# Encoder trunk: decay products one pair later, the second norm's gain and offset inside the output projection, and the first weight unit split in halves

## The reference, cut to what matters

```
proj = x @ W_in                      # q/k/v, z, beta, decay, window q/k/v, gates
branch A: centred conv (5 taps) + SiLU on q/k/v, L2-normed q/k,
          gated delta rule forward and backward, per-head gated norm
          beta = sigmoid(b);  g = -exp(a_log) * softplus(a + dt_bias), cumulated per chunk
branch B: windowed attention with rotary q/k and a sink
merged = sigmoid(gate_A) * (A @ W_A) + sigmoid(gate_B) * (B @ W_B)
x = LayerNorm(alpha * x + merged @ W_out)       # first norm, gain and offset ln1
x = LayerNorm(alpha * x + SwiGLU(x))            # second norm, gain and offset ln2
```

## Time and profile before

| | |
|---|---|
| runs | 2651.22, 2661.05, 2661.07 us |
| profiled execution | 2658.32 us, its span 2656.5 us, mean granted TensorE clock 0.974 |
| PE busy | 2421.4 us (91%), 14128 matmuls |
| DVE / ACT / POOL busy | 1272.7 / 762.7 / 1061.5 us |
| DMA | 169.72 MB, mean 64 GB/s |

### The profile page before, as it was taken

One profiled execution on the slowest core, in us unless ns is written; L12 is line 12 of the kernel. 1 busy time (PEld: TensorE's weight loads), 2 busy tenths in 40 slices (PEclk: granted clock), 3 DMA queues, 4 the chain that ended last, 5 costly groups with the idle time before them and its releaser, 6 DMA issues. The chain is left out here.

```text
span 2656.5 us, 35272 instructions
## 1 busy us (share of the span) xinstructions
PE 2421.4 (91%) x14128; PEld 1987.6 (75%) x14128; DVE 1272.7 (48%) x2262; ACT 762.7 (29%) x2050; POOL 1061.5 (40%) x612
## 2 busy tenths in 40 slices
PE   7988999987999989999989889999969999899997
PEld 5876777776887868888767677777758878788886
DVE  3667778756433251110257778787564432511102
ACT  2544444422332021110035344444223320211100
POOL 3541111142115646666635411111521156466665
PEclk8999999998999999999989899999989999899999
DMA  3220000021002323333212100000210032233332
GB/s 120 88 64 25 25 25 25 25 72 40 25 25 95 99 68 96 95 99 116 89 56 80 56 25 25 25 25 25 80 32 25 32 99 93 72 97 102 102 105 87
DMA packets 47249, 169.72 MB, mean 64 GB/s; under 512 B 5872, under 2 KB 6384, under 8 KB 46960
## 3 DMA queue, kind: packets, MB, share of 16 engines
q1 hardware_dynamic: 44496, 160.71, 19.3%
q10 hardware_dynamic: 2592, 6.76, 0.7%
HBM read 165.36 MB, written 2.10 MB: 63 GB/s over the span
## 5 line engine op out<-in xcount | busy, mean ns | idle before, releaser
L435 POOL TENSOR_SCALAR wh<-w_raw 128x1024 fp32r<-128x1024 f32 x300 | 325.5, 1085 | 1543.5 <-DMA w_raw<-stream 1543.5
L437 POOL TENSOR_TENSOR wl<-w_raw,wh 128x1024 fp32r<-128x1024 f32 x300 | 724.5, 2415 | 25.0
L462 PE MATMUL PS<-xh,wh 128*128 128x512 f32 x1472 | 610.6, 415 | 26.5 <-POOL wl L437 10.0
L464 PE MATMUL PS<-xl,wh 128*128 128x512 f32 x1472 | 583.0, 396 | 0.0
L463 PE MATMUL PS<-xh,wl 128*128 128x512 f32 x1472 | 581.5, 395 | 0.0
L462 PEld LDWEIGHTS PS<-xh,wh 128*128 128x128 f32 x1472 | 282.1, 192 | 79.3 <-POOL wl L437 14.6
L464 PEld LDWEIGHTS PS<-xl,wh 128*128 128x128 f32 x1472 | 280.9, 191 | 61.1
L463 PEld LDWEIGHTS PS<-xh,wl 128*128 128x128 f32 x1472 | 282.7, 192 | 48.5
L1420 DVE SCALAR_TENSOR_TENSOR conv_acc<-PS,cw,conv_acc 128x510 f32<-128x510 f32 x192 | 143.8, 749 | 122.4 <-ACT conv_acc L1019 117.1
L1787 DVE TENSOR_TENSOR hf<-sg,PS 128x512 f32<-128x512 f32 x44 | 30.2, 687 | 358.0 <-PE PS L464 358.0
L1684 DVE SCALAR_TENSOR_TENSOR x<-x,PS 128x1024 f32<-128x1024 f32 x12 | 14.6, 1219 | 292.3 <-PE PS L464 292.3
(11 more groups left out here) (258 smaller groups left out, 4391.8 us busy)
## 6 DMA issues: line engine op xcount, KB each, us to landing
w_raw<-stream SPq DMA_DIRECT2D x300, 512.0 KB, 3.5
ln_g<-ln_rows ACTq DMA_DIRECT2D x4, 512.0 KB, 4.3
ln_b<-ln_rows ACTq DMA_DIRECT2D x4, 512.0 KB, 5.4
out<-x SPq DMA_DIRECT2D x3, 512.0 KB, 2.6
cst<-consts ACTq DMA_DIRECT2D x1, 1216.0 KB, 13.0
x<-x_in SPq DMA_DIRECT2D x2, 512.0 KB, 5.5
x<-x_in ACTq DMA_DIRECT2D x2, 512.0 KB, 7.5
out<-x SPq DMA_DIRECT2D x2, 256.0 KB, 2.1
```

The costliest lines, as they stand in the source:

```text
L435: nc.gpsimd.tensor_scalar(wh[s][:], w_raw[s][:], 1.0, 1.0, ALU.mult, ALU.mult).then_inc(w_hi_done, 1)
L437: nc.gpsimd.tensor_tensor(wl[s][:], w_raw[s][:], wh[s][:].bitcast(F32), ALU.subtract).then_inc(split_done, 1)
L462: mm(o, ah, bh, start=first, stop=False)
L464: return mm(o, ah, bl, start=False, stop=last)
```

## The change

- SP loads `ba_raw` behind the third unit of a layer instead of ahead of the first, and POOL splits it there.
- POOL splits the very first unit in two halves; PE's `feature_pair` waits for each half, and for its second unit only at that unit's first step.
- The steps of the decays move: PE's turn from behind i = 1 to behind i = 2, PE's sums from behind i = 4 into i = 6 behind unit 0; DVE's inputs to i = 3, rates to 5, tables to 6, signs to 8; ACT's Exp to i = 4, Ln and Sigmoid to i = 5, exponents to i = 7.
- In `store_normed` ACT writes the first high part before it scales tile 2.
- The gain and offset of layer 0's second norm leave the pairs of layer 1 and run in one go behind layer 1's merge, before `norm(0)`. Their rows are loaded in front of layer 1's first norm; ACT waits for the eight operations and then loads the rows of that norm.

```diff
@@ SP
-                sp.dma_start(ba_raw[:], w_ba[l, :, :, :]).then_inc(ba_loaded, 16)
                 for u in range(l * UNITS, (l + 1) * UNITS):
                     s = u % SLOTS
+                    if u == l * UNITS + SLOTS:
+                        sp.dma_start(ba_raw[:], w_ba[l, :, :, :]).then_inc(ba_loaded, 16)
@@ POOL (the split of ba_raw becomes split_ba, otherwise as before)
+                    if u == l * UNITS + SLOTS:
+                        split_ba()
                     pool.wait_ge(loaded[s], u // SLOTS * 16 + 16)
                     settle(pool)
-                    nc.gpsimd.tensor_scalar(wh[s][:], w_raw[s][:], 1.0, 1.0, ALU.mult, ALU.mult).then_inc(w_hi_done, 1)
-                    pool.wait_ge(w_hi_done, u + 1)
-                    nc.gpsimd.tensor_tensor(wl[s][:], w_raw[s][:], wh[s][:].bitcast(F32),
-                                            ALU.subtract).then_inc(split_done, 1)
+                    parts = (slice(0, 512), slice(512, 1024)) if u == 0 else (slice(0, 1024),)
+                    for n, w in enumerate(parts):
+                        nc.gpsimd.tensor_scalar(wh[s][:, w], w_raw[s][:, w], 1.0, 1.0, ALU.mult,
+                                                ALU.mult).then_inc(w_hi_done, 1)
+                        pool.wait_ge(w_hi_done, u + n + 1 + (u > 0))
+                        nc.gpsimd.tensor_tensor(wl[s][:, w], w_raw[s][:, w], wh[s][:, w].bitcast(F32),
+                                                ALU.subtract).then_inc(split_done, 1)
@@ PE
-                pe.wait_ge(split_done, pair * 2 + s + 1)
+                pe.wait_ge(split_done, pair * 2 + s + 2)
@@ feature_pair, step(n, k)
+                    if first_pair == n == 0:
+                        pe.wait_ge(split_done, 1 if k < KT // 2 else 2)
+                    elif k == 0:
+                        unit_ready(first_pair, n)
@@ PE, pairs
                         qkv_turn(i - 1, s)
+                        if i == 6 and s == 0:
+                            decay_sums()
...
-                    if i == 1:
+                    if i == 2:
                         decay_inputs()
-                    if i == 4:
-                        decay_sums()
@@ ACT, store_normed
                 scaled(0)
+                high_part(0)
                 scaled(2)
-                high_part(0)
@@ ACT, pairs (decay_logs holds the Ln and the Sigmoid)
-                    if i == 3:
+                    if i == 4:
                         decay_curves()
-                    if i == 6:
+                    if i == 5:
+                        decay_logs()
+                    if i == 7:
                         decay_exponents()
@@ ACT, ahead of normed(0)
-                act.dma_start(ln_g[:], ln_rows[l, 0, :].partition_broadcast(P)).then_inc(ln_loaded, 16)
-                act.dma_start(ln_b[:], ln_rows[l, 1, :].partition_broadcast(P)).then_inc(ln_loaded, 16)
+                def norm_rows(l, n):
+                    act.dma_start(ln_g[:], ln_rows[l, n * 2, :].partition_broadcast(P)).then_inc(ln_loaded, 16)
+                    act.dma_start(ln_b[:], ln_rows[l, n * 2 + 1, :].partition_broadcast(P)).then_inc(ln_loaded, 16)
+                if l > 0:
+                    norm_rows(l - 1, 1)
+                    act.wait_ge(x_affine, (l * 2 - 1) * 8 + 8)
+                norm_rows(l, 0)
@@ ACT, ahead of normed(1): the loads of rows 2 and 3 become
+                if l == DEPTH - 1:
+                    norm_rows(l, 1)
@@ DVE, pairs
-                    if l > 0 and 3 <= i <= 6:
-                        output_gain(l - 1, 1, i - 3)
-                    if l > 0 and 7 <= i <= 10:
-                        output_offset(l - 1, 1, i - 7)
-                    if i == 2:
+                    if i == 3:
                         decay_inputs()
-                    if i == 3:
+                    if i == 5:
                         decay_rates()
-                    if i == 5:
+                    if i == 6:
                         decay_tables()
-                    if i == 6:
+                    if i == 8:
                         decay_signs()
-                    if i == 8:
                         key_norms()
@@ DVE, behind the merge
+                if l > 0:
+                    for c in range(CHUNKS):
+                        output_gain(l - 1, 1, c)
+                    for c in range(CHUNKS):
+                        output_offset(l - 1, 1, c)
                 norm(0)
```

More of the change, by code:

```diff
@@ L423, in _, with split_ba @@
             for l in range(0, DEPTH):
[L425 to L430, removed]
+                def split_ba():
+                    pool.wait_ge(ba_loaded, l * 16 + 16)
+                    settle(pool)
+                    flat = [t[:].rearrange("p k n -> p (k n)") for t in (ba_raw, bah, bal)]
+                    nc.gpsimd.tensor_scalar(flat[1], flat[0], 1.0, 1.0, ALU.mult, ALU.mult).then_inc(ba_split, 1)
+                    pool.wait_ge(ba_split, l * 2 + 1)
+                    nc.gpsimd.tensor_tensor(flat[2], flat[0], flat[1].bitcast(F32), ALU.subtract).then_inc(ba_split, 1)
                 for u in range(l * UNITS, (l + 1) * UNITS):
                     s = u % SLOTS
+                    if u == l * UNITS + SLOTS:
+                        split_ba()
                     pool.wait_ge(loaded[s], u // SLOTS * 16 + 16)
                     settle(pool)
-                    nc.gpsimd.tensor_scalar(wh[s][:], w_raw[s][:], 1.0, 1.0, ALU.mult, ALU.mult).then_inc(w_hi_done, 1)
-                    pool.wait_ge(w_hi_done, u + 1)
-                    nc.gpsimd.tensor_tensor(wl[s][:], w_raw[s][:], wh[s][:].bitcast(F32),
-                                            ALU.subtract).then_inc(split_done, 1)
+                    parts = (slice(0, 512), slice(512, 1024)) if u == 0 else (slice(0, 1024),)
[5 more added lines that the diff above has]
+                                                ALU.subtract).then_inc(split_done, 1)
             pool.wait_ge(ln_loaded, DEPTH * 64)
@@ L472, in feature_unit, with feature_pair @@
                 ins.then_inc(unit_done, 1)
-            def feature_pair(slots, lo_count):
+            def feature_pair(first_pair, lo_count):
+                slots = [slot_of(first_pair, n) for n in range(2)]
                 def step(n, k):
+                    if first_pair == n == 0:
+                        pe.wait_ge(split_done, 1 if k < KT // 2 else 2)
+                    elif k == 0:
+                        unit_ready(first_pair, n)
                     c = slice(k * P, (k + 1) * P)
@@ L565, in qkv_turn @@
                     ins.then_inc(tok_ready, 1)
-                feature_pair([unit_ready(l * PAIRS + AT_QKV, s) for s in range(2)], l * 16)
+                feature_pair(l * PAIRS + AT_QKV, l * 16)
                 pe.wait_ge(ready_bf, 7)
@@ L928, in _ @@
                         if i == j == 0:
-                            feature_pair([unit_ready(pair, s) for s in range(2)], l * 16 + 8)
+                            feature_pair(pair, l * 16 + 8)
                             continue
@@ L1000, in decay_curves, with decay_logs @@
                     A(sm[3][:], sm[2][:], ACT.Exp).then_inc(gate_act, 1)
+                def decay_logs():
                     act.wait_ge(gate_dve, l * 19 + 5)
@@ L1245, in _ @@
                           ACT.Copy).then_inc(ff_hi, 1)
-                act.dma_start(ln_g[:], ln_rows[l, 2, :].partition_broadcast(P)).then_inc(ln_loaded, 16)
-                act.dma_start(ln_b[:], ln_rows[l, 3, :].partition_broadcast(P)).then_inc(ln_loaded, 16)
+                if l == DEPTH - 1:
+                    norm_rows(l, 1)
                 normed(1)
```

## The result

The changed kernel took 2642.05 us as the median of 6 runs (2638.05 to 2647.63), the kernel before 2660.95 us beside it (6 runs, 2651.22 to 2665.48). The ratio is 0.9936, 95% interval 0.9920 to 0.9952: 17 us or 0.64% faster (18.9 us by the two medians). In two later jobs it gave 0.9919 (0.9902 to 0.9936) and 0.9928 (0.9903 to 0.9953). The forecast was 2644 us in a range of 2631 to 2655. So the sign, the time and the range held. One term of the sum, the burst, was wrong all the same, and losses that the sum did not have took its place.

What follows compares the result with a forecast made beforehand. PE, busy 91% of 2656.5 us, was taken as the bound, so only its gaps and the low clock behind them pay. 15.2 + 10.9 + 1.4 - 6.0 + 1.4 + 0.1 - 8.3 = 14.7 us below 2658.3 gave 2644, range 2631 to 2655.

Steps and rivals of the forecast that it cites:

- the burst: Layer 1's output projection: eight DVE products in one run hold POOL's subtraction off, PE stalls; 8.3 us lost.
- Decay turn: First stage, both layers: a pair later, PE's wait on `baT` and the low clock behind it vanish; 15.2 us saved.
- Gains out of the convs: Layer 1's convs: without gains and offsets its turns go as layer 0's; 10.9 us saved.
- Pair 4: Conv of pair 4, both layers: splitting ACT's three decay curves over two pairs ends its delay; 1.4 us saved.
- Decay sums: Pair 6, both layers: new 2.2 us wait before unit (6,1) plus 0.8 us for low clock; 6.0 us lost.
- Start: Kernel start: PE does six matmuls on the first half unit, then waits for unit 1; 1.4 us saved.
- Norm order: Three norms: first high part before the second scaling; earlier DVE subtraction waits longer for POOL; 0.1 us saved in all.
- rival (a): Output projection: POOL goes in between DVE's operations, so the 8.3 us loss goes; 2635 us, chance 0.30.
- the norm's run: Same eight operations behind the FFN's norm: POOL's operation took 2.54 us, starting at the run's end; evidence for the 8.3 us.
- the product row: Layer 1's convs: POOL's subtraction between two TMP products took only 2.68 us, so it went in between; evidence for (a).

Runs made afterwards that it cites:

- experiment 2: Changed kernel with the decay steps of PE, ACT and DVE back in their old places: 2648.56 us, 0.9958 of the kernel before.
- experiment 1: Changed kernel with the second norm's gains and offsets back in layer 1's convs, with their row loads: 2647.64 us, 0.9956 of the kernel before.
- experiment 4: Changed kernel with each layer's first norm's gains and offsets applied twice, sixteen DVE operations in one run: 2655.99 us, one execution.
- experiment 5: Changed kernel with DVE's run of eight in the output projection started only after POOL split the third weight unit: 2646.83 us, 0.9956 of the kernel before.
- job 2: Changed kernel run again unchanged, beside other versions on one chip: 2637.73 us median of 6 runs; profiled span 2631.2 us.
- job 3: Changed kernel run again unchanged, beside other versions on one chip: 2641.92 us median of 6 runs.
- Experiment 7: Changed kernel with DVE's last low part of the gated output moved behind the window copies: 2637.34 us, 0.9912 of the kernel before.

## Why the prediction was right, and where it was not

**Decay turn (15.2).** Right, in idle time and low clock: 7.6 and 7.8 us by the n-th matmul, 7.2 and 7.0 the other way round in experiment 2. It went whole, since nothing was late in its place.

**Gains out of the convs (10.9).** Right in mechanism and size: 5.6 + 5.8 = 11.4 in the first pair of traces, which holds pair 4 of layer 1 as well; 11.1 the other way round in experiment 1. Comparing layer 1 with layer 0 at the same place was what gave the number.

**Pair 4 (1.4).** 0.4 in layer 0, PE's wait of 0.43 us on the conv, for 0.7; within the sum above in layer 1.

**Decay sums (-6.0).** The wait was there in both layers, 1.88 and 1.82 us for 2.2. Low clock behind it did not come in this execution (1.00); in the two others of this kernel one short stretch followed in layer 0, none in layer 1. So 3.7 to 5 us for 6.0.

**Start (1.4).** PE began when foretold and waited until 17.93; 0.8 us was left, because the clock behind the new gap was 0.54. Over the three profiled executions of the changed kernel it was 0.8 to 2.2 us, over all twelve with this start 0.4 to 2.2.

**Norm order (0.1).** About nothing, as foretold. The first low part comes earlier and waits longer for POOL (2.55 for 1.99 us). PE's first unit behind the norms comes 0.5 us sooner in all than in before, from the last matmul ahead of each norm; 0.3 of this is layer 1's, where before lost time to low clock. Against the old order in the changed kernel it comes 0.2 us later in all. Both lie inside the bounds.

**The burst (-8.3).** This step failed. "POOL's subtraction waits from 2222.2 to 2231.2" and "PE stalls 5.9 us" did not come; DVE's eight operations took 19 us, POOL's operations 1 us more each, and PE lost 0.7 us at the last pair. It was rival (a)'s outcome. I had carried the behaviour of the earlier trace rows to another place because the operations were the same. They were, and experiment 4 shows that the behaviour in that place is real, with 11.58 us. But in the projection POOL gets its turn at each boundary, also when it comes in mid-run (experiment 5), and in the norm's run it never does. What makes the difference is open: operations, shapes and the phase of arrival are excluded by the two experiments. One difference stands in every trace and was not tried: POOL has idled for 16 to 17 us when it comes into the norm's run, and for some 2 us when it comes into the projection's. Nor was it tried what other engines do at the time. The Trainium skill, "SBUF — State Buffer", section "Who interferes with whom", says of DVE's two-port modes that whoever issues first has the shared pair "for the whole instruction", and of an instruction with two SBUF inputs that it contends with a POOL instruction that reads SBUF. If the first is taken to hold for these operations too, as the prediction took it, the projection agrees (2.1 and 3.24 us); the norm's run goes beyond it, and there the 11.58 us decide.

**Why 2644 was near all the same.** With the sizes measured, the terms make 15.4 + 11.4 + 0.4 - 3.7 + 0.8 + 0.5 - 0.7 = 24.1 us, which would be 2634 against the execution of 2658.3. The execution of job 2 did just this (25.3); the first execution was 11.6 us faster only, that of job 3 15.9. The medians were 18.9, 21.8 and 19.1 us below those of the kernel before beside them. So 2 to 5 us in the medians, and 12 in the first execution (1.6 in layer 0, 10.3 in layer 1), were lost to window waits and short stretches of low clock, which vary between executions of one kernel (spans of 2631.2, 2640.6 and 2645.0). The forecast had 8.3 us for a stall that did not come, and these losses, which it did not have, stand in its place. That makes its nearness in part luck. What shifts the losses between executions could not be settled. Experiment 7 removed the long window waits, and its median gained nothing clear of the scatter.

## What to carry to other kernels

Look at the same stage in another layer or pass that lacks the suspected work: the difference of two turns was a better price than any sum of waits. Before giving a wait's price to the total, ask whether a later wait hangs on another engine's chain (here `kg`), for it can take back part of what is saved ahead of it. To see what an order on another engine costs, measure from the last matmul ahead of the place to the first behind it, not the last idle time alone. And where two engines share a port, take both outcomes, turns and hold-off, as possible in a new place even for the same operations, and prefer the one that the place's own neighbours show: the product row was nearer than the norm's run.

## What was not expected of the hardware

- A run of DVE operations with two inputs in SBUF held POOL off for 10.5 us beyond its own 1.05 (11.58 us) in one place, and let it in at each boundary in another (1.1 to 2.12 us for the same rounding).
- DVE's subtraction took 0.69 us when it came 0.01 us ahead of POOL's, and 2.85 us when it came 0.07 us behind.
- A wait of 1.8 us in layer 1's first stage left the clock at 1.00, one of 3.60 at the start was followed by 0.54, one of 10.91 by 0.57. Short low stretches (2051.0 to 2054.4 in after, 0.51) also come in the attention, where PE's idle times around them are 0.3 to 1.04 us, and not in the same places in each execution; one costs PE 1.3 to 1.6 us.
- Executions of one kernel spread over 21 us (2627.37 to 2648.68), about what the whole change is worth.
